# Layers 0 and 1 of a four-layer transformer kernel: layer norms with the tokens on partitions, layer 0's two output products ahead of both feed-forwards, and another order of the opening's loads

## What is computed

```python
def layer_norm(x, g, b):
    mu = mean(x); var = mean(square(x - mu))            # over the 1024 features of a token
    return (x - mu) * rsqrt(var + 1e-6) * g + b

def swiglu(h, w_in, w_out):
    a, g = split(h @ w_in, 2)                           # 1024 -> 2 x 2816
    return (silu(g) * a) @ w_out                        # 2816 -> 1024

for l in range(2):
    sh1, sc1, g1, sh2, sc2, g2       = split(silu(c) @ ada_w[l] + ada_b[l], 6)      # latent
    csh1, csc1, cg1, csh2, csc2, cg2 = split(silu(c_ctx) @ ada_w[l] + ada_b[l], 6)  # context
    h, hc = x * (1 + sc1) + sh1, xc * (1 + csc1) + csh1
    y, yc = mixer[l](h, hc)          # projections, attention, pooling or convolution, @ w_out
    x = layer_norm(ALPHA * x + g1 * y, ln1_g[l], ln1_b[l])
    x = layer_norm(ALPHA * x + g2 * swiglu(x * (1 + sc2) + sh2, ffn_in[l], ffn_out[l]), ln2_g[l], ln2_b[l])
    if l == 0:                       # the context stream is carried through layer 0 only
        xc = layer_norm(ALPHA * xc + cg1 * yc, ln1_g[l], ln1_b[l])
        xc = layer_norm(ALPHA * xc + cg2 * swiglu(xc * (1 + csc2) + csh2, ...), ln2_g[l], ln2_b[l])
```

## Time and profile before

| | |
|---|---|
| median of 3 runs | 3293.58 us (3291.41 to 3293.84) |
| the profiled execution, its own time | 3292.36 us |
| its span, first to last instruction | 3290.4 us |
| TensorE matmul busy | 3127.8 us, 95% |
| TensorE weight loads busy | 2702.0 us, 82% |
| VectorE busy | 2074.9 us, 63% |
| ScalarE busy | 1239.0 us, 38% |
| GpSimd busy | 104.9 us, 3% |
| chain that ended last | TensorE 84%, VectorE 10%, ScalarE 2%, issue 1%, DMA 1% |
| mean granted TensorE clock | 0.976 of 2.4 GHz |

### The profile page before, as it was taken

How to read it: one execution, slowest core, us unless ns; L and a number is a source line. 1 busy time by engine, 2 the same in 40 slices (tenths; PEclk the granted TensorE clock), 3 DMA queues, 4 the chain that set the end, 5 groups by cost and what they waited for, 6 DMA issues and landing times.

```text
span 3290.4 us, 52352 instructions
## 1 busy us (share of the span) xinstructions
PE 3127.8 (95%) x20148; PEld 2702.0 (82%) x20148; DVE 2074.9 (63%) x3728; ACT 1239.0 (38%) x1884; POOL 104.9 (3%) x133
## 2 busy tenths in 40 slices
PE   6989998999989999898999999999899999999999
PEld 2558998986779978687999999887688899999887
DVE  1566556554456530678976666686669885666687
ACT  1244445441344421322444444432431444444433
POOL 0100000000000000022000000000013000000000
PEclk9999999999989999999999999999899999999999
DMA  6354543542445533243666666674244566666674
GB/s 259 135 182 128 186 166 128 185 153 96 156 161 185 185 128 115 77 133 124 231 230 224 206 206 207 223 242 155 67 145 140 182 225 230 207 222 207 201 251 163
DMA packets 190523, 579.70 MB, mean 176 GB/s; under 512 B 16768, under 2 KB 61824, under 8 KB 185760
## 3 DMA queue, kind: packets, MB, share of 16 engines
q1 hardware_dynamic: 185408, 542.15, 49.4%
q10 hardware_dynamic: 4608, 33.56, 2.4%
q0 software_dynamic: 352, 1.90, 0.2%
HBM read 542.94 MB, written 34.60 MB: 176 GB/s over the span
## 4 chain that ended last, share of the span: by engine, by line
PE 84%; DVE 10%; ACT 2%; issue 1%; DMA 1%; PEld 0%; POOL 0%; ACTq 0%; DVEq 0%; SPq 0%; PEldq 0%; POOLq 0%
PE ps L1108 28%; PE ps L1189 28%; PE ps L904 5%; PE ps L852 3%; PE ps L1406 3%; PE ps L1383 3%; PE ps L907 2%; PE ps L1098 2%; DVE w_split L2308 2%; PE ps L996 1%; PE ps L857 1%; PE ps L981 1%; PE ps L783 1%; DVE arena L2505 1%; DVE arena L2499 1%
## 5 line engine op out<-in xcount | busy, mean ns | idle before, releaser
L2308 DVE TENSOR_TENSOR w_split<-ring,w_split 128x1024 fp32r<-128x1024 f32 (+1 forms) x707 | 865.7, 1226 | 601.3 <-ACT w_split L1792 600.7
L1108 PE MATMUL ps<-x_split,w_split 128*128 128x256 f32 x8352 | 1058.2, 285 | 31.1 <-DVE w_split L2308 17.4
L1108 PEld LDWEIGHTS ps<-x_split,w_split 128*128 128x128 f32 x8352 | 1039.5, 193 | 53.4 <-issue 19.5
L1792 ACT ACTIVATE w_split<-ring 128x1024 fp32r<-128x1024 f32 (+1 forms) x707 | 746.4, 1058 | 739.0 <-PE ps L1189 453.2
L1189 PE MATMUL ps<-w_split,h_split 128*128 128x512 f32 (+1 forms) x4056 | 958.6, 390 | 3.6 <-DVE w_split L2308 2.9
L1189 PEld LDWEIGHTS ps<-w_split,h_split 128*128 128x128 f32 (+1 forms) x4056 | 748.6, 188 | 152.9 <-DVE w_split L2308 5.3
L1866 ACT ACTIVATE arena<-ps 128x256 f32<-128x256 f32 (+1 forms) x256 | 98.3, 385 | 499.0 <-PE ps L1108 412.1
L904 PE MATMUL ps<-arena,ring 128*128 128x512 f32 (+1 forms) x416 | 152.7, 524 | 10.9 <-DVE arena L2663 6.1
L904 PEld LDWEIGHTS ps<-arena,ring 128*128 128x128 f32 x416 | 81.3, 196 | 73.3 <-issue 68.0
L1383 PE MATMUL ps<-x,ring 128*128 128x256 f32 x608 | 140.0, 388 | 0.0
L852 PE MATMUL ps<-x,ring 128*128 128x256 f32 (+1 forms) x608 | 132.6, 380 | 0.3 <-DVE x L2234 0.3
(11 more groups left out here) (306 smaller groups left out, 2486.1 us busy)
## 6 DMA issues: line engine op xcount, KB each, us to landing
ring<-in_peer_u SPq DMA_DIRECT2D x256, 512.0 KB, 3.3
ring<-in_peer_v SPq DMA_DIRECT2D x256, 512.0 KB, 4.2
ring<-in_ffn_in SPq DMA_DIRECT2D x132, 512.0 KB, 3.3
ring<-in_ada SPq DMA_DIRECT2D x96, 512.0 KB, 5.5
ring<-in_ffn_out SPq DMA_DIRECT2D x66, 512.0 KB, 3.3
spread_rows<-arena ACTq DMA_DIRECT2D x32, 1024.0 KB, 3.9
arena<-spread_rows SPq DMA_DIRECT2D x20, 1536.0 KB, 8.2
ring<-in_pq SPq DMA_DIRECT2D x32, 512.0 KB, 3.3
```

The lines of the kernel that those rows point to most:

```text
L1108: last = mm(dst, w_split[:, w, wp, at:at + P], rhs[rp], start=(first and i == 0), stop=(final and i == 2), skip_group_check=shared)
L1792: f(w_split[0:rows, w, 0, :], ring[0:rows, slot, :], ACT.Copy).then_inc(w_high, 1)
L2308: v.tensor_tensor(w_split[0:rows, w, 1, :], ring[0:rows, slot, :], w_split[0:rows, w, 0, :].bitcast(F32), ALU.subtract).then_inc(w_low, 1)
```

## The change

Two `sums_at` places let two output products be summed without waiting for each other: `out00` in banks 4 to 7, everything else in banks 0 to 3. All ten norms of the program now have the tokens on partitions. In layers 0 and 1 the gated sum is still made with features on partitions (now from `x` directly, with the gates divided by `ALPHA` and the epsilon by `ALPHA` squared), then TensorE turns it (`turn_sums`, 16 transposes), `token_scaled` and `turn_normed` follow, `normed_kept` writes `x`, and `shifted_input` and `input_highs` (both on ScalarE) and `input_lows` make the feed-forward's input from `x`. Layer 0's order becomes `out00`, `out01`, `hidden00`, `hidden01`, with the pieces of each norm placed between tiles of the next product. The opening loads the small condition vectors first and the streams behind the 17th weight block; `modulate0` and `lambda` are no stages of their own any more.

```diff
-    for name, n in (("ident", P), ("mean_d", P), ("mean_64", P), ...
+    for name, n in (("ident", P), ("mean_64", P), ...
...
-           ("out00", "ab_out", 8), ("hidden00", "ffn0", 0), ("out01", "ab_out", 8), ("hidden01", "ffn0", 0)] + ...
+           ("out00", "ab_out", 8), ("out01", "ab_out", 8), ("hidden00", "ffn0", 0), ("hidden01", "ffn0", 0)] + ...
...
         def _(sp):
-            for dst, src in ((cond[:, :, :], a["cond"]), (x[:, CTX, :, :], a["ctx"]), (x[:, LAT, :, :], a["x"]),
-                             (params[:, :], a["params"]), (consts[:, :], a["consts"]), (gate_w[:, :, :], a["gate_w"])):
-                sp.dma_start(dst, src).then_inc(loaded, 16)
+            lo, hi = C_AT["pick"]
+            for dst, src in ((cond[:, :, :], a["cond"]), (consts[:, lo:hi], a["consts"][:, lo:hi])):
+                sp.dma_start(dst, src).then_inc(cond_loaded, 16)
...
+            stream(a["ada0"], R, 0)
+            sp.dma_start(params[:, :], a["params"]).then_inc(params_loaded, 16)
+            stream(a["ada0"], 2 * KD - R, R)
+            stream(a["ab_in"], 1, 0)
+            inputs()
...
                             if l == 1 and n == 0:
                                 pe.wait_ge(mod_ready, k + 1)
+                            if l == 0 and n == 0:
+                                pe.wait_ge(ctx_ready, k + 1)
+                                pe.wait_ge(lat_ready, k + 1)
...
-            def norm(name, between=None):
...
+            def turn_sums(name):
+
+                n = token_norm_of(name)
+                for c in range(2):
+                    pe.wait_ge(res_ready, KD * n + 4 * (c + 1))
+                    for r in range(2):
+                        for k in range(4 * c, 4 * c + 4):
+                            last = nc.tensor.transpose(ps[:, bank_of(name, r, c), (k % 4) * P:(k % 4 + 1) * P],
+                                                       res[:, k, r * P:(r + 1) * P], const("ident"))
+                        last.then_inc(res_turned, 1)
...
                 def go_out(t, ph, b, first=False, final=False):
+                    if first:
+                        token_x_ready(held, token_x_at("v")[-1])
+                        token_x_ready(held, token_x_at("a")[-1])
...
                 if l == 0:
-                    out_project(f"out0{CTX}", tiles(CTX))
-                    hidden(f"hidden0{CTX}", FH, 2, lambda: out_project(f"out0{LAT}", tiles(LAT), 0, 1))
-                    out_project(f"out0{LAT}", tiles(LAT), 1)
+                    enter(pe, "out00")
+                    out_project("out00", out_tiles(0, CTX))
+                    out_project("out01", out_tiles(0, LAT), {1: lambda: turn_sums("out00"), 4: lambda: turn_normed("out00")})
+                    hidden("hidden00", FH, 2, "out01", {0: turn_sums, 1: turn_normed})
+                    hidden("hidden01", FH, 2, "hidden00", {0: turn_back, 1: turn_sums, 2: turn_normed})
+                    turn_back("hidden01")
+                    turn_sums("hidden01")
+                    turn_normed("hidden01")
...
+            def shifted_input(name):
...
+                for k in range(KD):
+                    of, at = ("v", token_x) if k in token_x_at("v") else ("a", token_xa)
+                    act.wait_ge(at, before + token_x_at(of).index(k) + 1)
+                    f(h2[:, k, :], x[:, s, k, :], ACT.Identity, scale=mod[:, l, 4 * KD + k, j:j + 1],
+                      bias=mod[:, l, 3 * KD + k, j:j + 1]).then_inc(h2_ready, 1)
+
+            def input_highs(used):
...
+                    f(x_split[:, 0, k, :], h2[:, k, :], ACT.Copy).then_inc(x_high, 1)
...
+            def second_layer_rest():
+
+                enter(act, "out11")
+                out_highs("out11", out_tiles(1, LAT))
+                first_highs("hidden11", 0, 2)
+                load_root()
+                token_scaled("out11", by_token, 2)
+                normed_kept("out11")
+                shifted_input("out11")
+                input_highs(0)
+                first_highs("hidden11", 2)
...
-                chain(v.tensor_scalar(res[:, :, :], x[:, s, :, :], ALPHA, None, ALU.mult))
                 for k in range(KD):
                     complete(name, k)
-                    v.scalar_tensor_tensor(res[:, k, :], wide[:, k, :], mod[:, l, part_ * KD + k, j:j + 1],
-                                           res[:, k, :], ALU.mult, ALU.add).then_inc(res_ready, 1)
+                    v.scalar_tensor_tensor(res[:, k, :], wide_from[sums_at(name)][:, k, :], mod[:, l, part_ * KD + k, j:j + 1],
+                                           x[:, s, k, :], ALU.mult, ALU.add).then_inc(res_ready, 1)
...
+                out_lows("out11", out_tiles(1, LAT))
+                first_lows("hidden11", 0, 2)
+                gated_sum("out11")
+                token_scaled("out11", by_token)
```

518 lines of the change are left out of this document (287 added, 231 removed).

## The result

| | before | changed |
|---|---|---|
| median | 3292.49 us (3287.38 to 3293.84, 4 runs) | 3246.74 us (3245.87 to 3247.86, 4 runs) |
| profiled execution, span | 3292.36, 3290.4 | 3245.87, 3244.2 |
| TensorE busy | 3127.8 | 3097.2 |
| VectorE, ScalarE busy | 2074.9, 1239.0 | 2049.7, 1233.2 |
| mean granted clock | 0.976 | 0.979 |

The ratio is 0.9864, 95% interval 0.9851 to 0.9876. The change gained 45.8 us; the forecast was a gain of 34.3, to 3259.3 us, in a range whose fast end was 3248. The direction was right, the size was not, and the range was missed by 1.3 us. That the kernel would be faster by over 0.2% had been given a chance of 0.94, and it was.

What follows compares the result with a forecast made beforehand. TensorE, busy 95% of the span, was taken as the bound, with its stops at handovers between products and at the opening. Gains 8.6 - 0.65 + 24.0 + 3.7 - 3.45 + 2.1 = 34.3 gave 3259.3 us, range 3248 to 3272.

Steps and rivals of the forecast that it cites:

- The opening: Before TensorE's first product: inputs land 2.6 us earlier and modulation is handed over feature by feature, gain 8.6 us.
- The end of `project0`: Stage closing gets an `Exp` and three small VectorE operations, about 1.95 us, less a 1.28 load: -0.65.
- The crossing: From `out00`'s end to `hidden01`'s end: 47.8 us of norm cost falls to 23.8, a gain of 24.0.
- the prediction's own sign of being wrong: Forecast is wrong if `out00`'s end to `hidden01`'s end is not 422 us within 8.
- The stop ahead of `hidden00`: After `out01`, TensorE stops 4.2 us until VectorE's low parts are ready; bounds 0 and 13.2.
- The dip priced at 1.65: Lowered granted clock after the stop before `hidden00`: 4.2 x 0.39 = 1.65 us lost.
- The three handovers: `project1`, `hidden11` and the gates start 13.65, 16.6 and 12.6 us behind their products: gains 3.7, -3.45 and 2.1.
- Rival D: Some six small stops, each followed by a low-clock stretch costing 1.65 us: 3269 us, chance 0.08.
- B: In-order lists: waiting norm pieces delay splits; the stop before `hidden00` is 13.2 us, not 4.2: 3271 us, chance 0.15.
- C: Slower than before: all three inner norms stop TensorE, 15.4 us each: 3301 us, chance 0.03.
- E: At the opening, inputs land with the rest of the stream and only 3.5 us remain: 3264.4 us, chance 0.08.
- F: Full cover: no stop before `hidden00` and half the small ones gone: 3250 us, chance 0.06.

Runs made afterwards that it cites:

- `whole_modulate`: Changed kernel with TensorE waiting for all eight modulated features of both streams before the first product; 3250.77 us.
- `inputs_first`: Changed kernel with only SP's load order undone: streams, constants and gate weights ahead of the weight blocks again; 3251.15 us.
- the second profile: Changed kernel, unchanged, measured and profiled once more; 3245.24 us.
- `lambda_late`: Changed kernel with the scalar's `Exp` moved behind the entry to `attend0` and VectorE's two operations to the start of `out00`; 3244.88 us.
- `shift_shared`: Changed kernel with the shifted input of `out00` and `out11` made by VectorE and ScalarE, four features each; 3245.61 us.
- `norms_alone`: Changed kernel with the three inner norms (`out00`, `out01`, `hidden00`) no longer beside the next product; 3263.12 us.
- `before_warm_tail`: Kernel before the change with 14 extra transposes at the tail of `attend0`, where TensorE waits for ScalarE's copy; 3289.90 us, ratio 0.9996.

## Why the prediction was wrong, step by step

**What bounds the kernel** was read rightly as far as it goes: each stop named is where the chain changed. Three stretches with a low clock were not named: the tail of `attend0`, the gates' matmuls and the mLSTM.

**The opening**: forecast 8.6, measured 6.8 from the first profile and 8.3 from the second; the kernel before varies as well (first product at 42.04, in its second profile at 43.31). The bytes were counted rightly (inputs 32.8, measured 33.05 and 34.57; last condition block near 26.5, used at 26.83), and so was the hand-over (3.5, `whole_modulate` 3.7). That the scale "is no bound" held for the changed order; with the old order and the new hand-over it is the bound (`inputs_first`), which the split into two terms that add did not see.

**The end of `project0`**: forecast -0.65. Between the first product and `attend0`'s second pair of scores the second profile lost 0.6 (8.3 to 7.7). That term was right. Another 1.2 is lost inside `attend0`, which was not forecast and which I have not traced. `lambda_late` shows that the place of the `Exp` costs 2.7 up to the first scores.

**The crossing**: forecast 24.0, measured 445.6 - 420.4 = 25.2; the prediction's own sign of being wrong, 422 us missed by over 8, did not come. Tile 6 late 0.75, measured 0.91. The stop ahead of `hidden00` 4.2, measured 3.0 in two pieces, both ended by VectorE's low parts as named. The normed turn of `out01` late 1.05, measured 1.18. The dip priced at 1.65 is there: clock 0.50 from 299.95 to 303.36, and 7.15 us for the 45 matmuls that take 5.65 in `shift_shared` without it, 1.5 us. That the mean of the whole crossing reads 1.00 only says that 3.41 us are little in 420. The table load is 1.28 as forecast and no drain follows. The Trainium skill's 2.66 us for a switch ("ScalarE: Activation LUTs", What ACT_TABLE_LOAD costs) does not show in any row here.

**The three handovers**: `project1` 13.65 behind its product, measured 13.9; `hidden11` 16.6, measured 16.4; the gates 12.6, measured 12.6. These are terms from layer 2's norm, carried over row by row, and they are right to 0.3 us in the first profile. In the other profiles of changed kernels with the same code there, `hidden11` starts 16.4 to 17.1 behind its product and the gates 12.6 to 13.1.

**The step that failed** is the sum. It added the terms and let every other stage take what it took before. That term for the other stages was put at nothing, without a reason. Rival D priced the clock only as a loss, and only inside the crossing. What was left out: the profile of before had its clock down at the tail of `attend0` (0.64 over 19 us), in the gates and in the mLSTM (0.62 over 16 us), stages that the change leaves alone but reaches at other moments. The sum would have needed a term of 0 to 15 us for them, on the fast side. Measured were 5.1 + 2.3 + 7.1 = 14.5 (7.1 is the mLSTM's 7.8 less the 0.7 lost behind it), and with them the fast end of the range would have been at 3259.3 - 14.5 = 3244.8, not at 3248. Without them the change's own steps give 31.7 of the 34.3 forecast. No one could have said ahead which way these dips would go; that they could go was to be read from the rows.

**The rivals**: B, C, D, E and F all fell. C failed twice: the cover works, and without it a norm costs 6 us on average and not 15.4, as `norms_alone` shows. D's series of dips in the crossing was one dip. F's 3250 is the nearest to the measured time, but by luck: the stop that it denies is there, 3.0 us.

## What to carry to other kernels

Before a change is priced, list the stretches of the old profile with a granted clock under 1, wherever they lie: each is a gain or a loss that a shift of one to three microseconds ahead of it, or another execution, can switch, and the range must hold it. Judge a repair by the chain up to a landmark behind it, not by the median alone; here 5.7 us were hidden by a clock dip some 130 us later. And look at a place in every profile that has the same code up to it before a gain there is put down to an edit: the 2.4 us of `before_warm_tail` came without its transposes too. A cost carried over row by row from the same construction elsewhere in the program (the token norm of layer 2) held to 0.3 us in three places.
